# Last norm, token rows and expert routing in one block of instructions, with the raw logits' products ahead of the token tiles

## The reference, cut to what matters

```python
def rms_norm_2(x, g):
    return x * lax.rsqrt(jnp.mean(x * x, axis=-1, keepdims=True) + EPS) * g

# end of second_block
h = rms_norm_2(x, norm_ffn[l]) * (1.0 + scale_f) + shift_f
y = hier_moe(h.reshape(bsz * s, d), w_group[l], b_group[l], w_router[l], b_router[l], w_gate[l], w_up[l], w_down[l])
x = x + gate_f * y.reshape(bsz, s, d)

def hier_moe(h, ...):
    group_logits = h @ w_group + b_group                        # 4 groups
    g_sel = argmax(group_logits);  p_group = softmax(group_logits)[g_sel]
    exp_logits = (h @ w_router + b_router)                      # 32 experts, 8 to a group
    top_p, top_i = top_k(softmax(exp_logits[g_sel]), 2)
    weights = p_group * top_p / sum(top_p)
    # slots: an expert's tokens stand together, padded to blocks of 128;
    # 16 + 32 = 48 blocks at most; slot_tok lists the token of each slot
    xb = h_pad[slot_tok].reshape(n_blocks, 128, d)
    yb = (silu(xb @ w_gate[e]) * (xb @ w_up[e])) @ w_down[e]    # for each block
    y = segment_sum(yb * slot_w, slot_tok)
```

## Time and profile before

| | us |
|---|---|
| median of 3 runs (4586.13 to 4586.83) | 4586.62 |
| the profiled execution: its span | 4584.7 |
| median above that span | 1.9 |
| of it, from the first weight prefetch (3672.14) to the first turned expert rows (3851.18) | 179.04 |
| TensorE busy over the span | 3953.7 (86%) |

### The profile page before, as it was taken

How to read it: one execution, slowest core, us unless ns; L and a number is a source line. 1 busy time by engine, 2 the same in 40 slices (tenths; PEclk the granted TensorE clock), 3 DMA queues, 4 the chain that set the end, 5 groups by cost and what they waited for, 6 DMA issues and landing times. The chain is left out here.

```text
span 4584.7 us, 42478 instructions
## 1 busy us (share of the span) xinstructions
PE 3953.7 (86%) x16276; PEld 2819.4 (61%) x16276; DVE 2099.5 (46%) x2655; ACT 1550.5 (34%) x2451; POOL 673.8 (15%) x332
## 2 busy tenths in 40 slices
PE   4799799999798799996857899889999855999996
PEld 1687455568586355583636666567777744666664
DVE  0391466651372566622356423233442213666665
ACT  1412345550422445413141335222220012555542
POOL 0221200002221100020101010123333222011111
PEclk9899899999899799987988899999999966999997
DMA  4211100111210121222312110233333234999975
GB/s 165 74 37 30 35 19 29 32 42 65 78 47 26 42 66 56 65 83 53 40 40 52 45 21 10 42 75 83 88 86 68 74 112 129 359 352 358 353 290 213
DMA packets 346632, 451.05 MB, mean 98 GB/s; under 512 B 51965, under 2 KB 221106, under 8 KB 344898
## 3 DMA queue, kind: packets, MB, share of 16 engines
q1 hardware_dynamic: 331186, 405.28, 29.3%
q0 software_dynamic: 12656, 25.26, 1.5%
q10 hardware_dynamic: 2592, 17.83, 1.0%
HBM read 408.39 MB, written 59.31 MB: 102 GB/s over the span
## 5 line engine op out<-in xcount | busy, mean ns | idle before, releaser
L1144 PE MATMUL values<-probs,vp 128*128 128x512 f32 x672 | 348.6, 600 | 12.0 <-issue 6.4
L1232 ACT ACTIVATE probs<-scores 128x512 f32<-128x512 f32 (+1 forms) x336 | 196.0, 583 | 306.3 <-PE scores L219 304.6
L217 PE MATMUL scores<-q_hi,k_rest 97*128 97x512 f32 (+1 forms) x336 | 262.3, 781 | 0.0
L3382 PE MATMUL dp<-h_t,abt 128*128 128x512 f32 x544 | 241.9, 598 | 1.1 <-ACT abt L3431 0.9
L261 POOL TENSOR_TENSOR ring_r<-ring_w,ring_hi 128x1024 fp32r<-128x1024 f32 x44 | 136.8, 3111 | 702.5 <-ACT ring_hi L254 702.5
L3413 ACT ACTIVATE expert_hi<-wu 128x1024 fp32r<-128x1024 f32 x136 | 144.8, 1065 | 251.4 <-PE gp L219 251.4
L1313 DVE TENSOR_REDUCE mx<-made 128x1 f32<-128x640 f32 (+1 forms) x272 | 203.9, 794 | 27.2 <-PE made L1085 26.4
L217 PE MATMUL smb<-x_t_r,merge_w_r 128*128 128x512 f32 x480 | 196.1, 408 | 22.2 <-POOL merge_w_r L2723 19.4
L217 PE MATMUL gates_ps<-x_t_r,ring_r 128*128 128x512 f32 (+1 forms) x560 | 206.5, 369 | 2.5 <-PEq L83 2.5
L734 DVE SCALAR_TENSOR_TENSOR conv_out<-conv_in,vectors,conv_out 128x1295 f32<-128x1295 f32 (+1 forms) x120 | 205.9, 1716 | 4.3
L218 PE MATMUL gates_ps<-h_t_r,ring_hi 128*128 128x512 f32 (+1 forms) x560 | 206.4, 369 | 0.0
(11 more groups left out here) (527 smaller groups left out, 9504.9 us busy)
## 6 DMA issues: line engine op xcount, KB each, us to landing
wg<-in_w_gate SPq DMA_DIRECT2D x34, 2048.0 KB, 9.8
wu<-in_w_up SPq DMA_DIRECT2D x34, 2048.0 KB, 11.0
h_t<-in_w_down SPq DMA_DIRECT2D x34, 2048.0 KB, 9.9
ahead_w<-in_w_ada SPq DMA_DIRECT2D x48, 512.0 KB, 3.9
ring_w<-in_w_in SPq DMA_DIRECT2D x44, 512.0 KB, 4.0
mod_w<-in_w_mod ACTq DMA_DIRECT2D x8, 1536.0 KB, 29.1
ahead_w<-in_w_mod SPq DMA_DIRECT2D x24, 512.0 KB, 3.5
out_w<-in_w_out SPq DMA_DIRECT2D x24, 512.0 KB, 5.2
```

The source lines that it names most:

```text
L217: nc.tensor.matmul(out, lhs[1], rhs[0], start=start, stop=False, **kw)
L1144: nc.tensor.matmul(O[b % 2][:, 0:w], vp[g // 2 % 2][:, kb, g % 2 * VD:g % 2 * VD + P], pr[m % 3][:, 0:w], start=kb == 0, stop=kb == nk - 1 ...
L1232: nc.scalar.activation(pr[m % 3][:, 0:w], S[m % 2][:, 0:w], ACT.Exp, scale=scale).then_inc(s.exped, 1)
L3382: m = nc.tensor.matmul(dp[half][:, :], at[:, j, :], wd[u][:, j, half * 512:(half + 1) * 512], start=j == 0, stop=j == FK - 1)
```

## The change

One function `ffn_route` takes the place of `norm_factors`, `rms_modulate`, `turn_out` and `route` here, with one block and one barrier. The norm is factored out of the logits: with r the token's root and f the channel's factor, logits = r * (x @ (f * W)) + shift @ W + b. So:

- SP loads the routers' inputs first, then the expert weights, stores the token rows, and then loads the down weights.
- PE spreads shift and factor over the partitions, makes the raw logits with the scaled weights as stationary operand and 512 tokens moving, turns the token tiles, makes the constant part, and turns the raw logits.
- For each token tile ACT squares and sums in one instruction (`accum_out`) and takes the root on one column; DVE makes the normed rows from the turned tile, POOL adds the shift rows, SP stores.
- The counts use fp32r copies of the one-hot rows and 16 products in place of 44.
- The table of slots is made in PSUM by 16 products of one-hot matrices, so the DRAM table, its 16 scatters and its reload are gone. POOL's fills of `xb` and of the pad column move here too.

```diff
-def route(nc, k, a, r):
+def ffn_route(nc, k, a, r, mod, shift_at, scale_at):
...
@@ block.sync
+            for u in range(2):
+                for dst, src, sem in ((r.wg[u], a.w_gate_2, r.gate_in[u]), (r.wu[u], a.w_up_2, r.up_in[u])):
+                    sp.dma_start(dst[:, :, :], src[0, u].rearrange("(k p) n -> p k n", p=P)).then_inc(sem, 16)
+            for t in range(T):
+                sp.wait_ge(s.shifted, t + 1)
+                sp.dma_start(r.rows[t * P:(t + 1) * P, :], rows[:, t, :]).then_inc(s.stored, 16)
+            sp.wait_ge(s.stored, 16 * T)
+            for u in range(2):
+                sp.dma_start(r.wd[u], a.w_down_2[0, u].rearrange("(k p) n -> p k n", p=P)).then_inc(r.down_in[u], 16)
@@ block.gpsimd
+                nc.gpsimd.tensor_tensor(rows[:, t, :], rows[:, t, :], s_rows[:, :], ALU.add).then_inc(s.shifted, 1)
@@ block.tensor
+            def turn_tile(t):
+                if t >= 2:
+                    pe.wait_ge(s.rowed, t - 1)
+                for j in range(DK):
+                    m = nc.tensor.transpose(x_ps[t % 2][:, j * P:(j + 1) * P], k.x[:, j, CTX + t * P:CTX + (t + 1) * P],
+                                            k.ident)
+                m.then_inc(s.turned, 1)
+            def raw_logits(j):
+                for b in range(2):
+                    m = nc.tensor.matmul(raw_ps[:, b, :], fw[:, j, :], k.x[:, j, CTX + 512 * b:CTX + 512 * (b + 1)],
+                                         start=j == 0, stop=j == DK - 1)
+                m.then_inc(s.raw_made, 1)
...
+            pe.wait_ge(s.kept1, 1)
+            pe.wait_ge(s.weighted, 1)
+            for j in range(DK):
+                raw_logits(j)
             for t in range(T):
-                for j in range(DK):
-                    m = nc.tensor.matmul(lg_ps[:, t, :], k.h[:, j, CTX + t * P:CTX + (t + 1) * P], w[:, j, :],
-                                         start=j == 0, stop=j == DK - 1)
+                turn_tile(t)
...
+            nc.tensor.matmul(rank_ps[:, :, :], before_r[:, :], both[:, :, :], start=True, stop=False)
+            for d in range(1, T):
+                nc.tensor.matmul(rank_ps[:, d:T, :], ones_r[:, :], both[:, 0:T - d, :], start=False, stop=d == T - 1)
...
+            for n in range(CH):
+                if n % T == 0:
+                    pe.wait_ge(s.places_ready, 2 if n else 1)
+                m = nc.tensor.matmul(table_ps[:, :, :], lane[:, n, :], blocks_r[:, n, :, :], start=n == 0, stop=n == CH - 1)
@@ block.scalar
+            for t in range(T):
+                act.wait_ge(s.turned, t + 1)
+                nc.scalar.activation(lane_f[:, 0:DK, :].rearrange("p a b -> p (a b)"), x_ps[t % 2], ACT.Square,
+                                     accum_out=ss[:, t:t + 1]).then_inc(s.squared, 1)
+                act.wait_ge(s.squared, t + 1)
+                step(nc.scalar.activation(ss[:, t:t + 1], ss[:, t:t + 1], ACT.Ln, bias=k.eps, scale=1.0 / D))
+                nc.scalar.activation(rt[:, t:t + 1], ss[:, t:t + 1], ACT.Exp, scale=-0.5).then_inc(s.rooted, 1)
+            act.wait_ge(s.raw_made, DK)
+            nc.scalar.activation(raw[:, :], raw_ps.rearrange("p a b -> p (a b)"), ACT.Copy).then_inc(s.raw_kept, 1)
@@ block.vector
+            for t in range(T):
+                dve.wait_ge(s.rooted, t + 1)
+                V.scalar_tensor_tensor(rows[:, t, :], x_ps[t % 2], rt[:, t:t + 1], f_rows[:, :], ALU.mult, ALU.mult)\
+                    .then_inc(s.rowed, 1)
...
+            dve.wait_ge(s.table_made, 1)
+            V.tensor_scalar(r.idx[:, 0:NB, :], table_ps.rearrange("p c b -> p b c"), float(2 * SEQ), None, ALU.add)\
+                .then_inc(r.table_in, 1)
@@ block.gpsimd (route, before)
-            for i in range(2):
-                for t in range(T):
-                    pool.indirect_dma_start(r.table, bass.IndirectOffsetOnAxis(ap=r.slot[:, i, t:t + 1].bitcast(U32), axis=0),
-                                            tok[:, t, 2 * i:2 * i + 2], None).then_inc(s.scattered, 16)
@@ second_block
-            prefetch_experts(nc, k, a, r)
-            norm_factors(nc, k, factor, "norm_ffn", mod, 4 * DK, 2)
-            rms_modulate(nc, k, X_BLOCKS, factor, mod, 3 * DK)
-            turn_out(nc, k, k.h, CTX, r.rows)
-            route(nc, k, a, r)
+            ffn_route(nc, k, a, r, mod, 3 * DK, 4 * DK)
             experts(nc, k, a, r)
```

More of the change, by code:

```diff
@@ L613, in _ @@
                     .then_inc(s.biased, 1)
[L616 to L654, removed]
 def conv_segments(blocks):
@@ new lines, in _ @@
+            for u in range(2):
+                sp.dma_start(r.wd[u], a.w_down_2[0, u].rearrange("(k p) n -> p k n", p=P)).then_inc(r.down_in[u], 16)
+        @block.gpsimd
+        def _(pool):
+            nc.gpsimd.memset(r.idx[:, NB:NB + 1, :], 2 * SEQ).then_inc(r.pad_set, 1)
+            for u in range(2):
+                nc.gpsimd.memset(r.xb[u][:, :], 0.0).then_inc(r.pad_set, 1)
+            for t in range(T):
+                if t == 0:
+                    pool.wait_ge(s.kept1, 1)
+                pool.wait_ge(s.rowed, t + 1)
+                nc.gpsimd.tensor_tensor(rows[:, t, :], rows[:, t, :], s_rows[:, :], ALU.add).then_inc(s.shifted, 1)
@@ new lines, in raw_logits @@
+            def raw_logits(j):
[4 more added lines that the diff above has]
+            for j in range(DK):
+                m = nc.tensor.transpose(s_ps[:, j * P:(j + 1) * P], shift[:, j, :].broadcast_to([P, P]), k.ident)
+            m.then_inc(s.spread1, 1)
+            pe.wait_ge(s.factored, 1)
@@ new lines, in _ @@
+            for j in range(DK):
+                m = nc.tensor.transpose(f_ps[:, j * P:(j + 1) * P], factor[:, j:j + 1].broadcast_to([P, P]), k.ident)
+            m.then_inc(s.spread0, 1)
+            pe.wait_ge(s.kept1, 1)
+            pe.wait_ge(s.weighted, 1)
+            for j in range(DK):
+                raw_logits(j)
+            for t in range(T):
+                turn_tile(t)
+            pe.wait_ge(s.kept0, 1)
+            for j in range(DK):
+                m = nc.tensor.matmul(const_ps, shift[:, j, :].broadcast_to([P, P]), w[:, j, :], start=j == 0, stop=j == DK - 1)
@@ L3084, in _ @@
             for t in range(T):
-                for i in range(t + 1):
-                    m = nc.tensor.matmul(rank_ps[:, t, :], k.mats[:, BEFORE, :] if i == 0 else k.ones[:, :],
-                                         both[:, t - i, :], start=i == 0, stop=i == t)
-            for t in range(T):
-                m = nc.tensor.matmul(cnt_ps[:, :], k.ones[:, :], both[:, t, :], start=t == 0, stop=t == T - 1)
-            m.then_inc(s.ranks_made, 1)
+                m = nc.tensor.matmul(cnt_ps, ones_r[:, :], both[:, t, :], start=t == 0, stop=t == T - 1)
@@ L3235, in two @@
                 return [sb(f"{n}{u}", shape, dt) for u in range(2)]
[L3237 to L3239 removed]
+            wd, idx, xb = r.wd, r.idx, r.xb
             ix, sx = two("ix", [P, 1], I32), two("sx", [P, 1], I32)
             w_hi = sb("expert_hi", [P, RING, 2, FF], F32R)
[L3242 removed]
             x_hi, x_rest = sb("x_hi", [P, DK, P], F32R), sb("x_rest", [P, DK, P], F32R)
@@ L3257, in _ @@
             def _(sp):
-                with nc.allow_non_contiguous_dma("a column of indices to each block"):
-                    sp.dma_start(idx[:, 0:N_BLOCKS, :], r.table.rearrange("(b p) o -> p b o", p=P)).then_inc(s.table_in, 16)
                 def load(dst, src, e, sem):
@@ L3594, in second_block @@
     r.rows = nc.dram_tensor("token_rows", [SEQ, D], F32, kind="Internal").ap()
-    r.table = nc.dram_tensor("slot_table", [N_BLOCKS * P, 2], I32, kind="Internal").ap()
     r.out_rows = k.slot_rows
```

166 lines of the change are left out of this document (105 added, 61 removed).

## The result

| | kernel before | changed kernel |
|---|---|---|
| median, us | 4586.61 | 4476.42 (4469.88 to 4482.75) |
| ratio, 95% interval | | 0.9758 [0.9744, 0.9771] |
| profiled span | 4584.7 | 4467.9 |
| first DMA issue of the stretch to the first turned expert rows | 179.04 | 78.69 |
| the span behind these rows | 733.5 | 732.4 |

What follows compares the result with a forecast made beforehand. No engine bounds the stretch, a chain of short stages with barriers; the expert loop behind is full. 99.0 earlier plus 3.9 for the gather is 102.9 of 179.04; span 4481.8, plus 1.9, gives 4484, range 4476 to 4499.

Steps and rivals of the forecast that it cites:

- Opening: Start of the new block: routers' loads land 4.87 us after first issue, weights scaled in 0.46; raw logits start at 3677.6.
- Raw logits: 32 TensorE instructions at 0.425, 13.6 us, plus 1.7 for half clock at the start; all 15.3 on the path.
- Rival A: Raw logits at half clock throughout: 27.2 us in place of 15.3, 11.9 more, 4496; chance 0.07.
- Tiles: Turning and norming token tiles: 4.7 us per pair, 2.35 a tile, paced by ACT, DVE and turning.
- Port: DVE's routing chain waiting on the SBUF port shared with POOL's last shifts: 1.2 us charged.
- rival B: `accum_out` costing 0.5 a tile and POOL's shifts holding DVE's routing steps: 6 to 15 us more, 4490 to 4499; chance 0.17.
- Slots, table, last steps: From counts to the barrier: small steps 0.6, slots 6.2, table products 1.7 + 0.3, reading 0.3, six last steps 1.2.
- Barrier: Between DVE's last steps and the first gather: 0.74 us, priced from ScalarE's start after SP's prefetch issue.
- Gather: First gather of expert rows: 3.9 us in place of 7.81, with the down weights in before it; bounds 0 and 4.6.
- rival E: Gather waits on POOL, stores or down weights ending last, not DVE's chain: 4500 to 4530; chance 0.02.
- D: Slower than before: expert loop's loads come late, from 3.0 us a block more; 4603 at 3.5 a block; chance 0.01.
- Rival C: Chain shorter than forecast: tiles 1.2, no port wait 1.2, fp32r products 1.7, gather 0.7, clock 1.0; 4478; chance 0.11.

Runs made afterwards that it cites:

- mixed kernel: Changed kernel with TensorE turning token tiles 0 and 1 first, then alternating raw products of one channel chunk with one tile's turning; 4464.3 us, ratio 0.9744.

## Why the prediction missed

The step that failed is "I build the new stretch on the clock of the old one, from 3672.14". It took the code ahead as fixed, a term of nothing without a reason. By the table above that code ends sooner in a program with so many fewer instructions, 7.4 by the profiles' starts, and the ratios give 7.6 outside the stretch. With 4586.6, 100.4 saved in the stretch, 7.4 ahead of it and 1.1 behind, the sum is 4477.7, where the two groups of runs of the changed kernel have 4476.4 and 4479.0. With the instructions put back the changed kernel takes 4485.7 by its ratio, and 4586.6 less 100.4 is 4486.2: there the step holds.

That the time still came out at the range's edge is in part luck: the block gave 2.5 less than forecast and the code ahead over 7 more. The range gave the code ahead no width; its lower end was built from the block's terms alone. The first executions of the kernel before suggested none, as they agree within 0.7; the later ones of the same kernel spread from 4578.1 to 4596.3.

Inside the block, against the times after the first issue:

- *Opening*: forecast 5.5, measured 6.6; the routers' loads landed 1.1 us later than in the earlier trace rows.
- *Raw logits*: 15.3, measured 15.6. Clock 0.89 on the mean: TensorE had stood idle for 4.22, the clock fell as the products began, and was full from 3668 on. Rival A (half clock throughout) did not occur.

```profile
3663.41:3666.00 2.59, 2.59 (x4) 0.67 (x5) 0.49 (x3) 0.00 (x0) 0.00 (x0) 0.55 1.02 399
3668.00:3679.00 11.00, 11.00 (x27) 2.78 (x26) 0.00 (x0) 0.00 (x0) 0.00 (x0) 1.00 1.04 387
```

- *Tiles*: 2.35 a tile forecast and 2.35 measured (ACT's squares start at 3680.06 and, seven tiles later, at 3696.50), and from the raw products' end to the logits 21.9 and 21.83. ACT needed 1.7 a tile instead of 1.6: `accum_out` adds an instruction of 0.19, and the step with Ln took 0.29. The logits' +44.0 instead of +42.7 comes from the two terms above.
- *Port*: 1.2 charged, 0.46 found. The row L3184 took 0.92 while POOL's last shift ran until 3701.92, and 0.46 in the mixed kernel, where no shift was open. One shift was still open, not two or three, and `accum_out` cost 0.19 a tile, not 0.5, so rival B did not occur; its terms add up to 6 to 13 more, not to 15. The 1493 ns of the earlier trace rows are a mean of unlike rows: ten of the 16 operations took 0.69, as did those with an operand in PSUM, and the six that started while a POOL operation ran took 1.36 to 4.02. In this one, of the kernel before, DVE ends 0.55 behind POOL:

```profile
3361.04 3.49 POOL L2720 TENSOR_TENSOR merge_hi<-merge_w,ones 128x1536 fp32r<-128x1536 f32 x1 [9.80 <-DMA merge_w<-in_w_branch]
3363.72 1.36 DVE L2979 TENSOR_TENSOR merge_sg<-merge_sg,merge_prev 128x512 f32<-128x512 f32 x1
```

So such an operation is not slow in itself, and what it pays is the rest of the POOL instruction that it meets. That agrees with the Trainium skill (SBUF — State Buffer, SBUF: two separate sides), which calls the shared port pair an exclusive lock for the whole instruction.

- *Chain and counts*: `both`'s products at +53.0 for +52.4; counts 3.7, forecast 3.7.
- *Slots, table, last steps*: 15.2 (3713.53 to 3728.69), forecast 5.2 + 0.6 + 6.2 + 2.0 + 0.3 + 1.2 = 15.5.
- *Barrier*: 0.74 charged, 2.15 measured from DVE's last step to POOL's gather. The barrier in the earlier trace rows was followed by an ACT instruction; here POOL leads, and what takes it 1.4 longer no row shows.
- *Gather*: 3.9, measured 4.68, down from 7.81.

Together 102.9 became 100.35. The down weights' cover held: they were issued at 3704.57, 26 us ahead of the gather, and their packets ended near 3717, so rival E did not occur; nor did D, for the loop kept its pace. Rival C's figure came nearest to the measured time, but for another reason: of its terms only one (the port, by 0.7) went its way.

## What to carry to other kernels

Sum a change's terms from the stretch, but give the unchanged rest a width of its own: here a program with some 70 fewer TensorE instructions ran the code ahead of the edit about 7 us sooner, and a padded copy shows this apart from the edit. Before a mean is used as a price, look at the single rows behind it. Products that need nothing from a chain of two engines belong between its steps, not ahead of it. A load issued behind a full queue holds a barrier as surely as work does.

## What the runs showed of the hardware that was not expected

- The DMA engines' time for the same 13.63 MB is 17.7 to 18.1% or 19.7 to 19.9% of the stretch, by how many instructions the whole program has (on TensorE 16204 and fewer, or 16276 and more), though those of that stretch are the same.
- Eight fp32 turnings took 1.09 each time at granted clock 1.00 when raw products of 512 columns stood between them, and from 1.09 to 1.97 in the changed kernel, where they stand alone and the granted clock is 0.70 on the mean. The Trainium skill (TensorE: Matmul & The Clock Gate, Part 4: PE-mode transpose) says that full clock does not engage for transposes; the turnings here at 1.09 and 1.11 ran at full clock, so the rule is not borne out for fp32.
- A sum over 1024 columns by ACT costs an instruction of 0.19 beside the operation itself.
- The first gather took 4.68 from issue to use with the DMA queues idle, and 7.81 beside 4 MB of weights.
